# Scan rates made once for all tiles in the front, and each step's rows loaded by one repeated DMA

## What is computed

```python
cum = jnp.cumsum(dt * a, axis=2)                 # running sum inside a chunk, per head
last = cum[:, :, -1]
xdt = x * dt[..., None]
states = jnp.einsum('bcsgn,bcsgrp->bcgrpn', bm, xdt * jnp.exp(last[:, :, None] - cum)[..., None])
def step(carry, inp):
    st, dec = inp
    return carry * dec[..., None, None] + st, carry
final, prev = lax.scan(step, init_state, (states, jnp.exp(last)))
diff = cum[:, :, :, None] - cum[:, :, None, :]
lmat = jnp.exp(jnp.where(causal, diff, -jnp.inf))
cb = jnp.einsum('bclgn,bcsgn->bclsg', cm, bm)
y_diag = jnp.einsum('bclsgr,bcsgrp->bclgrp', cb[..., None] * lmat, xdt)
y_off = jnp.einsum('bclgn,bcgrpn->bclgrp', cm, prev) * jnp.exp(cum)[..., None]
```

## Time and profile before

| | us |
|---|---|
| median of 3 runs | 3415.24 |
| lowest and highest run | 3410.34, 3423.82 |
| span of the profiled execution | 3413.0 |
| PE busy in it | 3160.0 (93%) |
| DVE, ACT, POOL busy | 1559.8, 1009.8, 525.1 |
| front, channel products | 2015.5 to 2164.1 |
| scan, opening steps | 2164.2 to 2194.3 |
| scan, whole steps | 2194.3 to 2395.7 |

### The profile page before, as it was taken

How to read it: one execution, slowest core, us unless ns; L and a number is a source line. 1 busy time by engine, 2 the same in 40 slices (tenths; PEclk the granted TensorE clock), 3 DMA queues, 4 the chain that set the end, 5 groups by cost and what they waited for, 6 DMA issues and landing times. The chain is left out here.

```text
span 3413.0 us, 52595 instructions
## 1 busy us (share of the span) xinstructions
PE 3160.0 (93%) x19496; PEld 2216.1 (65%) x19496; DVE 1559.8 (46%) x3170; ACT 1009.8 (30%) x2323; POOL 525.1 (15%) x639
## 2 busy tenths in 40 slices
PE   6999989999987999999999799899899299999996
PEld 4888856667435788787887565666664155555553
DVE  3212178778654010101101254566785666666565
ACT  4111156755330111101111152235554222222222
POOL 0010235110100101011110120254101101111112
PEclk9999999999987999999999899999999599999998
DMA  6336353053639977787777630100414589999996
GB/s 231 130 108 114 92 188 113 20 132 95 241 132 339 352 267 250 244 275 245 265 255 262 232 121 1 56 22 28 112 33 173 197 293 334 326 335 339 338 335 257
DMA packets 340390, 672.38 MB, mean 197 GB/s; under 512 B 84041, under 2 KB 133065, under 8 KB 334017
## 3 DMA queue, kind: packets, MB, share of 16 engines
q1 hardware_dynamic: 308384, 568.00, 47.9%
q0 software_dynamic: 13616, 47.32, 5.5%
q10 hardware_dynamic: 18240, 55.16, 4.3%
HBM read 585.65 MB, written 90.97 MB: 198 GB/s over the span
## 5 line engine op out<-in xcount | busy, mean ns | idle before, releaser
L2756 PE MATMUL experts_gu_ps<-experts_xT,experts_wg 128*128 128x160 f32 x2048 | 301.3, 300 | 2.6 <-DVE experts_xT L2630 2.6
L2756 PE MATMUL experts_gu_ps<-experts_xT,experts_wu 128*128 128x160 f32 x2048 | 299.4, 299 | 0.0
L2756 PEld LDWEIGHTS experts_gu_ps<-experts_xT,experts_wg 128*128 128x128 f32 x2048 | 287.9, 191 | 9.9 <-issue 9.9
L2756 PEld LDWEIGHTS experts_gu_ps<-experts_xT,experts_wu 128*128 128x128 f32 x2048 | 285.6, 190 | 0.0
L2653 DVE TENSOR_TENSOR experts_hid<-experts_sil,experts_gu_ps 128x160 f32<-128x160 f32 x128 | 41.1, 321 | 516.1 <-ACT experts_sil L2584 516.1
L2722 PE MATMUL experts_y_ps<-down_ahead_wd,experts_hid 128*128 128x512 f32 x512 | 228.3, 599 | 0.0
L2584 ACT ACTIVATE experts_sil<-experts_gu_ps 128x160 f32<-128x160 f32 x128 | 38.9, 304 | 604.9 <-PE experts_gu_ps L2756 604.9
L2722 PEld LDWEIGHTS experts_y_ps<-down_ahead_wd,experts_hid 128*128 128x128 f32 x512 | 94.6, 190 | 114.4 <-issue 113.7
L3458 PE MATMUL front_pb_ps<-kept_hT,front_ahead_w 128*128 128x512 f32 (+1 forms) x384 | 138.7, 521 | 0.7 <-DVE kept_dt L3509 0.7
L3167 PE MATMUL experts_w_ps<-experts_wd,experts_hT 128*128 128x512 f32 x256 | 130.8, 597 | 8.5 <-issue 7.8
L3167 PE MATMUL experts_v_ps<-experts_wd,experts_hT 128*128 128x512 f32 x256 | 129.6, 592 | 0.0
(11 more groups left out here) (561 smaller groups left out, 6308.7 us busy)
## 6 DMA issues: line engine op xcount, KB each, us to landing
experts_wg<-in_l_w_gate SPq DMA_DIRECT2D x64, 2048.0 KB, 8.5
experts_wu<-in_l_w_up SPq DMA_DIRECT2D x64, 2048.0 KB, 12.7
down_ahead_wd<-in_l_w_down SPq DMA_DIRECT2D x32, 2048.0 KB, 10.6
experts_wd<-in_l_w_down SPq DMA_DIRECT2D x32, 2048.0 KB, 7.7
down_ahead_wd<-in_l_w_mod SPq DMA_DIRECT2D x16, 1024.0 KB, 9.2
proj<-proj_ob ACTq DMA_DIRECT2D x60, 256.0 KB, 2.3
first_w<-in_l_w_in SPq DMA_DIRECT2D x6, 2048.0 KB, 10.1
attn_a_mod_w<-in_l_w_mod ACTq DMA_DIRECT2D x12, 1024.0 KB, 6.5
```

Of the source, the lines that this page charges most:

```text
L2756: mm = nc.tensor.matmul(GU[f % 2][:, part, 0:N], w[:, h, k, c * P:(c + 1) * P], xT[:, k, :], start=(k == 0), stop=(k == KD - 1))
```

## The change

`Kept` no longer holds `da` but four arrays of the same size: `ncum` (negated running sums), `wdt`, `ec` and `dec`. They are made in `front` for all tiles and both directions: after channel block 0 PE makes the running sums (two products of 80 columns) and the totals (one of 160); before block 1 DVE takes ncum, dec and wdt from PSUM; after block 2's pad copies ACT makes the three exponentials; at block 3 PE transposes the 128 columns of ncum that belong to the 8 token tiles; ACT copies them out after block 4's pad copies, DVE multiplies wdt with dt, and SP stores the 128 x 128 values to a DRAM array `sums` before the stage ends. `u` moves into the space of `gate`.

In `scan` the `CR` products, the small running-sum product, the DVE function `sums` and ACT's three small exponentials are gone. xw is made from x and `wdt` directly, so that `xdt` is wanted in whole steps only. For every whole step SP issues one DMA that repeats a row of 4 KB from `sums` over 128 partitions into `ex[:, d]` (512 KB), when the m before the last is done (`load_row`); the eight absolute values then work in place. The query half of `w` is loaded in two parts of 1 MB, each followed by one of the first two rows; loads of keys and rope tables for later tiles stand between the row loads in SP's order. The two banks that `CR` leaves free go to a second fill bank: a fill waits for the bank's use two fills ago.

```diff
@@ front @@
+                sp.wait_ge(sums_act, START + 2)
+                sp.dma_start(sums, sums_row).then_inc(stored[NT % 4], 16)
...
+                    if c == 2:
+                        act.wait_ge(lw_done, START + 1)
+                        nc.scalar.activation(dec[:], dec[:], ACT.Exp)
+                        nc.scalar.activation(ec[:], ncum[:], ACT.Exp, scale=-1.0)
+                        nc.scalar.activation(wdt[:], wdt[:], ACT.Exp).then_inc(sums_act, 1)
+                    if c == 4:
+                        act.wait_ge(sums_pe, START + 2)
+                        nc.scalar.activation(sums_row, row_ps, ACT.Copy).then_inc(sums_act, 1)
...
+                def running_sums():
+
+                    pe.wait_ge(rates_ready, START + 2)
+                    by_direction = lambda v: v.rearrange("p (t d h) -> p d t h", t=NT, d=2)
+                    rates = by_direction(da[:].rearrange("p t r -> p (t r)"))
+                    for d in range(2):
+                        nc.tensor.matmul(by_direction(cum_ps)[:, d], tri[:, d, :], rates[:, d], start=True, stop=True)
+                    nc.tensor.matmul(tot_ps, tri[:, 0, P - 1:P].to_broadcast([P, P]), da[:].rearrange("p t r -> p (t r)"),
+                                     start=True, stop=True).then_inc(sums_pe, 1)
...
+                    if c == 0:
+                        running_sums()
+                    if c == 3:
+                        pe.wait_ge(lw_done, START + 1)
+                        nc.tensor.transpose(row_ps, ncum[:, 0:NTX, :].rearrange("p t r -> p (t r)"), K.ident[:]).then_inc(sums_pe, 1)
...
+                    if c == 1:
+                        dve.wait_ge(sums_pe, START + 1)
+                        flat = lambda v: v[:].rearrange("p t r -> p (t r)")
+                        link(nc.vector.tensor_scalar(flat(ncum), cum_ps, -1.0, None, ALU.mult))
+                        link(nc.vector.tensor_copy(flat(dec), tot_ps))
+                        link(nc.vector.tensor_tensor(wdt[:], dec[:], ncum[:], ALU.add))
+                        dve.sem_inc(lw_done, 1)
+                    if c == 4:
+                        dve.wait_ge(sums_act, START + 1)
+                        link(nc.vector.tensor_tensor(wdt[:], wdt[:], dt[:], ALU.mult))
@@ scan @@
-                for s, first in ((1, 0), (0, Z0)):
-                    sp.dma_start(w[:, s], w_rows[:, :, first:first + BANK]).then_inc(w_sem[s], 16)
+                def load_row(i):
+
+                    d, t = place(whole_steps[i])
+                    first = t * 2 * H8 + d * H8
+                    after(sp, m_done, i - 1)
+                    sp.dma_start(ex[:, d].rearrange("p h l -> p (h l)"),
+                                 row(sums[first:first + H8, :].rearrange("h l -> (h l)"), H8 * P)).then_inc(row_in[d], 16)
+
+                def load_q(half):
+                    some = slice(half * KD // 2, (half + 1) * KD // 2)
+                    sp.dma_start(w[:, 1, some], w_rows[:, some, 0:BANK]).then_inc(q_half_in[half], 16)
+
+                for i in range(2):
+                    load_q(i)
+                    load_row(i)
+                sp.dma_start(w[:, 0], w_rows[:, :, Z0:Z0 + BANK]).then_inc(z_in, 16)
...
-                for t in range(2, NTX):
-                    load_k(t)
+                for i in range(2, len(whole_steps)):
+                    load_row(i)
+                    kind, t = FILLS[max(i - 4, 0)]
+                    if i >= 4 and kind == "q" and t + 2 < NTX:
+                        load_k(t + 2)
...
-                    nc.scalar.activation(dec[:, d, :], last[:, d, :], ACT.Exp)
...
+                        act.wait_ge(row_in[d], START + 16 * (wholes[n] // 2 + 1))
                         for h in range(H8):
-                            a = nc.scalar.activation(ex[:, d, h, :], CR[:, h, :], ACT.Abs, bias=ncum[:, d, h:h + 1])
+                            a = nc.scalar.activation(ex[:, d, h, :], ex[:, d, h, :], ACT.Abs, scale=-1.0, bias=rate(kept.ncum, n)[:, h:h + 1])
...
-                    link(nc.vector.tensor_tensor(xw[:], xdt[:, d], per_head(wst[:, d, :]), ALU.mult))
+                    link(nc.vector.tensor_tensor(xw[:], by_head(kept.xb[:, t, 0:INNER]), per_head(rate(kept.wdt, n)), ALU.mult))
...
-                    if n + 1 < STEPS:
+                    if n + 1 < STEPS and whole(n + 1):
                         scaled(n + 1)
...
-                    for h in range(H8):
-                        nc.tensor.matmul(CR[:, h, :], rate(da, n)[:, h:h + 1].to_broadcast([P, P]), tri[:, d, :], start=True, stop=True)
...
-                        after(pe, f_out, f)
+                        after(pe, f_out, f - 1)
```

More of the change, by code:

```diff
@@ L3228, in __init__, with front @@
         self.dt = sb("dt", [P, NT, 2 * HEADS_D])
-        self.da = sb("da", [P, NT, 2 * HEADS_D])
+        self.ncum, self.wdt, self.ec, self.dec = (sb(v, [P, NT, 2 * HEADS_D]) for v in ("ncum", "wdt", "ec", "dec"))
         self.tri = sb("tri", [P, 2, P])
-def front(nc, K, kept, first, res, proj, moe):
+def front(nc, K, kept, first, res, proj, moe, sums):
     SLOTS = FrontAhead.SLOTS
@@ L3413, in _ @@
                 act.wait_ge(cw_in, START + 16 * (TAPS + 1))
-                for t in range(NT):
+                for t in range(AGAIN):
                     act.wait_ge(x_out[t], START + 16)
+                act.wait_ge(others_out, START + 16 * (NT - AGAIN))
                 for c in range(CHANNELS):
@@ L3558, in _, with scan @@
                     dve.sem_inc(taps_done, 1)
-def scan(nc, K, kept, w_in, proj, d_skip, gnorm_g, rope, out, following):
+def scan(nc, K, kept, sums, w_in, proj, d_skip, gnorm_g, rope, out, following):
     H8 = HEADS_D
@@ L3592, in scan @@
     order = [ends[n] for n in sorted(ends)]
+    whole_steps = [n for n in range(STEPS) if whole(n)]
     with Stage(nc, "scan") as st:
         w = st.sb("w", [P, 2, KD, BANK])
-        dt, da, tri = kept.dt, kept.da, kept.tri
+        dt, tri = kept.dt, kept.tri
         xdt = st.sb("xdt", [P, 2, H8, HD])
         xw = st.sb("xw", [P, H8, HD])
-        ncum = st.sb("ncum", [P, 2, H8])
-        lw = st.sb("lw", [P, 2, H8])
-        last = st.sb("last", [P, 2, H8])
-        wst = st.sb("wst", [P, 2, H8])
-        ec = st.sb("ec", [P, 2, H8])
-        dec = st.sb("dec", [P, 2, H8])
         cbm = st.sb("cbm", [P, GROUPS_D, P])
@@ L3841, in normed @@
                     v.then_inc(o_done, 1)
-                scaled(0)
-                sums(0)
                 done = 0
@@ L3864, in heads @@
                     col = conv_column(t)
-                    if n >= 1:
-                        pe.wait_ge(lw_done, START + n)
-                        after(pe, abs_done, wholes[n])
-                    if n >= 2:
-                        after(pe, cbm_done, wholes[n - 1])
-                    for h in range(H8):
-                        nc.tensor.matmul(CR[:, h, :], rate(da, n)[:, h:h + 1].to_broadcast([P, P]), tri[:, d, :], start=True, stop=True)
-                    for g in range(GROUPS_D if whole(n) else 0):
-                        nc.tensor.matmul(CB[d][:, g * P:(g + 1) * P], kept.bc[:, g, col:col + P], kept.bc[:, GROUPS_D + g, col:col + P], start=True, stop=True)
-                    nc.tensor.matmul(CB[d][:, GROUPS_D * P:GROUPS_D * P + H8], tri[:, d, :], rate(da, n), start=True, stop=True).then_inc(cum_done, 1)
+                    if not whole(n):
+                        return
+                    after(pe, cbm_done, wholes[n] - 1)
+                    for g in range(GROUPS_D):
+                        mm = nc.tensor.matmul(CB[d][:, g * P:(g + 1) * P], kept.bc[:, g, col:col + P], kept.bc[:, GROUPS_D + g, col:col + P], start=True, stop=True)
+                    mm.then_inc(cb_done, 1)
                 def states(n):
@@ L3940, in trunk @@
     skewed, lines = dram("skewed", (GRID * (BIASES * LINE + 1),)), dram("lines", (len(BIAS_BLOCKS) * COLS_IN, 8 * BIAS_LINE))
+    sums = dram("sums", (2 * HEADS_D * NTX, P))
     rope = (t["rope_cos"], t["rope_sin"])
@@ L3965, in trunk @@
                     with following:
-                        front(nc, K, kept, following, res, projs[n], moe)
+                        front(nc, K, kept, following, res, projs[n], moe, sums)
                     band_ahead = BandAhead(nc, K, projs[n])
-                    scan(nc, K, kept, layer["w_in"], projs[n], layer["d_skip"], layer["gnorm_g"], rope, mixed, band_ahead)
+                    scan(nc, K, kept, sums, layer["w_in"], projs[n], layer["d_skip"], layer["gnorm_g"], rope, mixed, band_ahead)
                 mix_ahead = MixAhead(nc, K, n, layer["w_out"], layer["w_router"], SEQ, mixed)
```

75 lines of the change are left out of this document (35 added, 40 removed).

## The result

The changed kernel takes 3374.9 us in the median of four runs (3372.8 to 3377.4), the kernel before 3414.8 (3410.3 to 3423.8): ratio 0.9877, with an interval of 0.9866 to 0.9889. The profiled execution of the changed kernel has a span of 3375.7 us, 37.3 less than before's; its own time of 3377.4 is the slowest of the four.

A forecast was written before the change was run, and what follows sets the result against it. PE's work was taken to bound the whole steps, the DVE-PE chain the opening steps. Terms -26.8 - 14 + 0.8 = -40 us; 3413.0 - 40 + 2.2 = 3375 us, range 3363 to 3390.

The forecast's parts named there:

- Whole steps: Scan: 14 steps lose 1.98 us of PE products each, 12.84 to 10.86 us; less 0.9 us of late stalls, -26.8 us.
- a wait of 0.2 us at the last step: Scan's last step: the second projection bank takes this PE wait away, but xw is later there anyway.
- Opening: Scan's four opening steps: xw starts at once from rates made in the front; first fill at 15.5 us, not 30.1; -14 us.
- The 1.8 us for a slow first fill: Opening: about 1.8 us taken off the gain for a first fill that runs at half speed.
- the 12.8 and the 18.8 of the two ends: Opening's gain: 12.8 us with PE's clock at 0.50 throughout, 18.8 us with the clock up all along.
- rival (3): Opening: PE's clock comes up early, first fill after 11.3 us, kernel 3370 us; chance 0.15.
- Front: Front's channels: three added PE products and one transpose cost 0.8 us (0.4 to 2); DVE's and ACT's additions are covered.
- Row transfer: Whole steps: one 512 KB DMA per step lands in about 4 us and costs nothing.
- The room of 14.7 us: Row transfer in whole steps: the landing may take 14.7 us before it costs anything.
- (1): Whole steps: DVE, slowed by POOL, or ACT holds PE in most steps; about 3389 us; chance 0.09.
- (2): Whole steps: chain over the row transfer binds; landing 14.7 to 23 us, chance 0.04; above 23, over 0.5% slower, chance 0.03.
- (4): A later stage gives the gain back or the products weren't on the path; about 3413 us; chance 0.03.

The follow-up runs named there:

- before_no_rows_two: Kernel before without its eight row products from step 6 on, with two fill banks and row space for four heads read twice: 3395.5 us.
- one_bank: Changed kernel with one fill bank instead of two: 3375.2 us.
- warm: Changed kernel with idle PE products at the front's end and between the opening's state products: 3371.1 us.
- pe_back: Changed kernel with 4 or 8 idle products of 128 columns ahead of the score products in 14 steps: 3385.0 us with 4, 3399.5 with 8.
- before_no_rows: Kernel before without its eight row products from step 6 on, DVE's and ACT's sums kept: 3402.2 us, ratio 0.9956.
- one_bank_late: Changed kernel with one fill bank and the row transfer some 10 us later: 3414.7 us in one execution.
- row_16us_later: Changed kernel with the row transfer waiting for the output sum of the step just before, 16.7 us later: 3395.8 us, ratio 0.9942.
- norm_late: Changed kernel with DVE normalising a finished tile after the next step's xw instead of before it: 3371.3 us in one execution.
- row_10us_later: Changed kernel with the row transfer waiting for the m of the step just before, 10.8 us later: 3373.2 us in one execution.

## Why the prediction was right, step by step

**Whole steps: -26.8 forecast, -26.86 found.** PE's work is the price, as the back-to-back rows said. The step is 10.83 for 10.86. Three late steps are 0.42 us longer than a plain one where I had 0.3, through the mechanism named, xw behind the normalising. The two small misses cancel (14 x 0.03 against 3 x 0.12), so the agreement to 0.1 us is luck; the mechanism is not. After's timeline of one such step:

```profile
2324.54 2.82 DVE L3882 SCALAR_TENSOR_TENSOR band_ahead_o<-scan_total,scan_ms,scan_gn 128x256 f32<-128x256 f32 x2
...
2327.28 0.68 DVE L3842 TENSOR_TENSOR scan_xw<-kept_xb,kept_wdt 128x512 f32<-128x512 f32 x1
...
2328.16 1.10 PE L3925 MATMUL scan_st_ps<-scan_xw,kept_xb 128*128 128x256 f32 x4 [0.19 <-DVEq L3843]
```

What the prediction did not see: in the kernel before, the products' time was to be had only together with either the second bank (before_no_rows_two) or the sums' removal (one_bank). It saw the bank only as a wait of 0.2 us at the last step, looked for the next limit in DVE's and ACT's idle time, and never asked how long before each fill the bank came free. The sum came out because the change removes that chain as well.

**Opening: -14 forecast, -14.90 found, less 1.07 in the first whole step.** The chain is as forecast at the low clock: state product 2.05 us (I had 2.0), 3.9 us from one to the next, first fill 15.2 us after the start (15.5). The 1.8 us for a slow first fill were booked in the opening; they lie in the first step and were 1.1. With them the change's two lines make -13.8, between the 12.8 and the 18.8 of the two ends, close to the low one. The clock did stay low, and for that the prediction had 12.8. The chain took 0.3 us less and the slow fill 0.7 less than it booked; the 1.2 us that it added for an early clock, which did not come, hides both. So the mechanism held, and the nearness of -14 is luck. Warm measured the other end: 11.1 us, where rival (3) had 11.3. That the rest of the opening's gain is the sums' work was read from the timelines; no run put that work back. How fast the clock rises is not fixed: of the eight traces with the changed opening and no idle products in it, five took 15.2 us to the first fill and three 13.9.

**Front: +0.8 forecast, +0.83 found.** PE's timeline has the three products 0.72 us from first to the next channel's, and one transpose of 0.11 (2089.29 to 2089.40). The timelines of PE and, for the exponentials, of ACT:

```profile
2033.73 0.57 PE L3487 MATMUL front_tp_ps<-kept_ncum,kept_tri 128*128 128x80 f32 x4
2034.14 0.48 PE L3488 MATMUL front_tp_ps<-kept_ncum,kept_tri 128*128 128x160 f32 x2
...
2071.62 1.28 ACT L3438 ACT_TABLE_LOAD   x1
2072.91 0.34 ACT L3438 ACTIVATE kept_dec<-kept_dec 128x160 f32<-128x160 f32 x1
...
2079.04 0.60 ACT L3400 ACTIVATE front_pad<-front_pb_ps 128x512 f32<-128x512 f32 x1 [5.34 <-DVEq L3595]
```

The next pad copy still waits 5.34 us for DVE (7.44 in the earlier trace rows), so the work was covered. The Trainium skill (ScalarE: Activation LUTs, What ACT_TABLE_LOAD costs) has a drain of 1.38 us on top of each load; here, as in the earlier trace rows, the load starts 0.02 us behind the instruction ahead of it and the next one 1.29 us after the load's start, so the measurement decides against it.

**Row transfer: about 4 us at no cost, found 3.6.** The view of the tile scan_ex and the DMA issues of the steady steps:

```profile
DMA to landing us min/median/max: 3.3/3.6/9.2
...
scan_ex<-sums SPq DMA_DIRECT2D x12, 512.0 KB, 3.6
```

The 9.2 us is one of the first two, amid the weight loads. The room of 14.7 us fits both runs: 3.6 + 10.8 = 14.4 us was still free, with DVE waiting 2.3 us for it in three steps and PE in none, and 3.6 + 16.7 = 20.3 was not. By the Trainium skill (DMA: Bandwidth & Descriptors, Anatomy of one DMA) the estimate was 3.2 us. That section gives its figures for DMAs that GpSimd issues, and these are issued by SyncE, which the prediction did not say; the trace is within half a microsecond all the same. The gate's 12.7 us was the queue, not the shape: in a quiet queue the same shape took 3.6.

**Rivals.** (1) fell with pe_back; (2) was reached only with the transfer 16.7 us later (its price was not tested, since that run makes a ring of one step and the prediction's is of two); (3) did not occur by itself; (4) is seen in one small form, the 1.7 us at the band's start, which comes and goes with the run.

## What to carry to other kernels

When work is taken off a back-to-back engine, look for the chain that is next in line before you count the gain: here it lay 3.1 us behind in plain steps and 0.75 in a late one, in a bank emptied by an engine that waited for a third, and work taken out of every step shortened that room twice. Two safeguards that each measure as worthless may cover one another (second bank, early issue), so undo them together before you drop either. And compare a small change by a stretch of the trace that holds the change and nothing else; the rest of this kernel scattered by more than 5 us.

## What the runs showed of the hardware

A short wait of PE can cost twice. In before_no_rows and one_bank_late the fill had nine waits of 1.6 to 6.2 us. Behind eight of them the next eight fill products took 5.3 to 6.5 us where they take 3.6, at a granted clock of 0.67 and 0.69 in the two such stretches read; behind one, of 2.56 us, they took 3.7. Behind the waits of 0.4 us they took 3.7, and behind the 1.4 us wait shown of row_16us_later the clock stayed at 1.00; behind its wait of 2.38 us for m the diagonal product took 3.68 us in place of 2.00, at 0.50. Idle products held it at 1.00 through the opening (warm), at no cost but PE's own free time.

ACT's eight absolute values take 2.44 us in place in SBUF with a scale of -1, and took 2.15 from PSUM without one; no run tells the two differences apart. DVE's xw takes 0.68 us alone and up to 1.65 with POOL's additions beside it (norm_late). The two operations of a normalising take 0.88 us by themselves (at the end of after's scan), 1.65 to 1.78 beside POOL's addition (row_10us_later), and 2.82 beside its addition and its multiplication (the late steps of after).
